# Odd layer of a two-block model: sums' reciprocals, head factors and logits by matmuls of high and low parts

## What is computed

```python
q = rms_norm(q.reshape(bsz, L, C_HEADS, C_HEAD_DIM), q_g)      # 8 heads of 128
k = rms_norm(k.reshape(bsz, L, C_KV_HEADS, C_HEAD_DIM), k_g)   # 2 heads of 128
...
logits = einsum('bqhgd,bqkhd->bqhgk', q_blk, k_sel) * (Dh ** -0.5)
logits = where(valid, logits + bias, NEG_INF)                  # bias by distance, per head
p = softmax(logits, axis=-1)
out = einsum('bqhgk,bqkhd->bqhgd', p, v_sel)
...
return (att * silu(gate)) @ w_out
```

## Time and profile before

| what | value |
|---|---|
| median of 3 runs | 2040.41 us (2038.06 to 2041.76) |
| the profiled execution's own time | 2038.71 us |
| its span | 2037.5 us |
| busy: PE, DVE, ACT, POOL | 97%, 70%, 43%, 32% |
| mean granted TensorE clock | 0.996 of full speed |
| odd attention, from the first logits' read to the last group | 833 to about 1016 us |

### The profile page before, as it was taken

How to read it: one execution, slowest core, us unless ns; L and a number is a source line. 1 busy time by engine, 2 the same in 40 slices (tenths; PEclk the granted TensorE clock), 3 DMA queues, 4 the chain that set the end, 5 groups by cost and what they waited for, 6 DMA issues and landing times.

```text
span 2037.5 us, 24547 instructions
## 1 busy us (share of the span) xinstructions
PE 1969.8 (97%) x9256; PEld 1515.3 (74%) x9256; DVE 1431.8 (70%) x2169; ACT 885.3 (43%) x1589; POOL 656.3 (32%) x476
## 2 busy tenths in 40 slices
PE   7999999999999999999999999999999999999997
PEld 6778766787648776666688777888787877778885
DVE  7667768513179997355427699899998887685539
ACT  5343366333356861344312333443326765362431
POOL 3677610452201211445444000000002673235443
PEclk9999999999999999999999999999999999999999
DMA  6322340342411122211053201121123213465322
GB/s 268 121 63 77 93 158 22 124 176 89 126 45 32 42 83 76 100 52 42 11 196 105 91 33 62 43 72 52 53 103 124 80 71 136 142 213 207 104 92 104
DMA packets 72431, 197.94 MB, mean 97 GB/s; under 512 B 11182, under 2 KB 20559, under 8 KB 71800
## 3 DMA queue, kind: packets, MB, share of 16 engines
q1 hardware_dynamic: 72168, 196.35, 28.1%
q10 hardware_dynamic: 144, 0.00, 0.0%
HBM read 152.89 MB, written 46.71 MB: 98 GB/s over the span
## 4 chain that ended last, share of the span: by engine, by line
PE 61%; DVE 19%; ACT 3%; issue 2%; POOL 1%; DMA 0%; DVEq 0%; ACTq 0%; SPq 0%
PE psum L266 58%; DVE m L2950 7%; PE psum L269 3%; DVE m L321 1%; DVE m L2971 1%; DVE m L2172 1%; DVE m L531 1%; DVE m L540 1%; DVE m L3149 1%; ACT m L301 1%; ACT m L395 1%; DVE m L3088 1%; DVE m L456 1%; DVE m L3152 1%; POOL m L311 0%
## 5 line engine op out<-in xcount | busy, mean ns | idle before, releaser
L266 PE MATMUL psum<-m,m 128*128 128x512 f32 (+9 forms) x8456 | 1886.9, 392 | 35.2 <-DVE m L321 9.5
L266 PEld LDWEIGHTS psum<-m,m 128*128 128x128 f32 (+3 forms) x8456 | 1429.0, 186 | 464.2 <-issue 145.1
L311 POOL TENSOR_TENSOR m<-m,m 128x1024 fp32r<-128x1024 f32 (+1 forms) x122 | 307.0, 2521 | 981.8 <-ACT m L301 981.5
L301 ACT ACTIVATE m<-m 128x1024 fp32r<-128x1024 f32 (+2 forms) x166 | 173.6, 1048 | 339.5 <-PE psum L266 214.9
L2950 DVE SCALAR_TENSOR_TENSOR m<-m,m,m 128x1024 f32<-128x1024 f32 x240 | 312.5, 1304 | 6.3
L269 PE MATMUL psum<-m,m 128*128 128x128 f32 x784 | 110.2, 276 | 19.3 <-ACT m L1446 6.0
L269 PEld LDWEIGHTS psum<-m,m 128*128 128x128 f32 x784 | 89.8, 141 | 39.9 <-ACT m L1446 8.0
L2172 DVE TENSOR_SCALAR_CACHE_REDUCE m<-m,m 128x896 bf16<-128x896 f32 (+4 forms) x130 | 102.8, 848 | 1.1
L2291 DVE CUSTOM_DVE_ANT_0 m<-psum,m 128x128 f32<-128x128 f32 (+3 forms) x64 | 48.3, 755 | 45.3 <-PE psum L266 22.8
L2386 ACT ACTIVATE m<-m,m 128x1024 bf16<-128x1024 f32 (+1 forms) x62 | 64.1, 1036 | 23.3 <-DVE m L2199 23.3
L2496 POOL TENSOR_TENSOR m<-m,m 128x384 f32<-128x384 f32 (+5 forms) x48 | 72.2, 1524 | 3.7 <-DVE m L2291 3.7
(11 more groups left out here) (308 smaller groups left out, 1663.0 us busy)
## 6 DMA issues: line engine op xcount, KB each, us to landing
m<-in_w SPq DMA_DIRECT2D x164, 512.0 KB, 3.4
scr_hscr<-m SPq DMA_DIRECT2D x4, 2048.0 KB, 6.6
m<-scr_hscr SPq DMA_DIRECT2D x4, 2048.0 KB, 10.5
scr_turned<-scr_strip SPq DMA_DIRECT2D x8, 575.5 KB, 12.3
m<-in_x SPq DMA_DIRECT2D x4, 1024.0 KB, 8.2
scr_gscr<-m SPq DMA_DIRECT2D x16, 256.0 KB, 4.3
m<-in_x SPq DMA_DIRECT2D x2, 2048.0 KB, 8.8
m<-scr_turned SPq DMA_DIRECT2D x8, 512.0 KB, 3.5
```

The source lines that it names most:

```text
L266: return self.nc.tensor.matmul(out, lhsT, rhs, start=start, stop=stop, skip_group_check=True)
L301: k.nc.scalar.activation(k.hi[SLOT[i]][:, 0:kk * n], k.raw[i % 2][:, 0:kk * n], ACT.Copy).then_inc(*k.up("w_hi", i))
L311: k.nc.gpsimd.tensor_tensor(lo, raw, hi.bitcast(F32), ALU.subtract).then_inc(*k.up("w_lo", i))
```

## The change

1. `norm`: `rs` is copied to fp32r into `RSP[0:64]`, and the rest goes to `RSP[64:128]`. `SEL` is the sum of two halves of the identity, so that one column picks a head's high and low rows at once. One fp32r matmul of all 128 partitions takes the place of the fp32 matmul of 10 partitions.
2. Reciprocals: DVE makes high and low parts of the four reciprocals (`RH`, `RL`) and multiplies the identity by each into `DG`, 128 x 512. PE multiplies a matrix of ones by both, two fp32r matmuls in place of four fp32 ones. `ONE` is written once by ACT.
3. Logits: `mm3` of high and low parts of queries and keys. ACT makes the high parts (`high_query`, one head ahead, 128 x 1024; `high_key`), DVE the low parts in place (`low_query`, `low_key`). A chunk of logits narrower than 256 columns is widened to 256.
4. Buffers: `pr[2]`, `strips[1]` move, and SP loads strip 1 after the last gate store and gate 0. DVE no longer waits for a gate store at unit (0, 2).

```diff
 # class Odd
+self.RSP, self.SEL = k.tile(H0 + 10 * KB, [512], F32R), k.tile(k.T0 + 512, [64], F32R)
+self.RH, self.RL = (k.tiny[:, o:o + 4] for o in (168, 172))
+self.QL, self.KL = self.MH, k.tile(PH + 32 * KB, [2, 1024], F32R)
 # tensor_odd, norm
-    hs = O.heads(half)
-    ins = k.mm(banks[half], k.ident[hs, hs.start + n:hs.start + n + 1].to_broadcast([10, 128]), O.rs[hs], True, True)
+    j = 32 * half + n
+    ins = k.mm(banks[half], O.SEL[:, j:j + 1].to_broadcast([128, 128]), O.RSP, True, True)
 # tensor_odd, s1
+pe.wait_ge(*at("q_lo", n))
+pe.wait_ge(*at("k_lo", kv))
 for c, e in O.chunks(b):
-    ins = k.mm(k.bank(bank + c // 512)[:, 0:e - c], O.QT[:, n, 128 * b:128 * b + 128], O.KT[:, n // 4, c:e], True, True)
+    e = max(e, c + 256)
+    ins = k.mm3(k.bank(bank + c // 512)[:, 0:e - c], (O.QH[n][:, bs], O.QL[:, n, bs]),
+                (O.KH[kv][:, c:e], O.KL[:, kv, c:e]), True, True)
 # tensor_odd, s3
-for i in range(4):
-    ins = k.mm(bank[:, 128 * i:128 * i + 128], O.recs[Q][:, i:i + 1].to_broadcast([128, 128]), k.ident, True, True)
+for i in range(2):
+    ins = k.mm(bank, O.ONE, O.DG[min(n, 1)][i].rearrange("p b q -> p (b q)"), i == 0, i == 1)
 # vector_odd
+def low_query(n):
+    dve.wait_ge(*at("q_hi", n))
+    V.tensor_tensor(O.QL[:, n], O.QT[:, n], O.QH[n].bitcast(F32), ALU.subtract).then_inc(*up("q_lo", n))
 if u == 18:
-    V.reciprocal(O.rs[0:64], O.rs[0:64]).then_inc(*up("head_rt"))
+    V.reciprocal(O.rs[0:64], O.rs[0:64]).then_inc(*up("head_rt", 0))
+    V.tensor_tensor(O.SEL, k.ident[:, 0:64], k.ident[:, 64:128], ALU.add).then_inc(*up("head_rt", 1))
+    V.tensor_copy(O.RSP[0:64], O.rs[0:64]).then_inc(*up("head_rt", 2))
+    V.tensor_tensor(O.RSP[64:128], O.rs[0:64], O.RSP[0:64].bitcast(F32), ALU.subtract).then_inc(*up("head_rt"))
 # vector_odd, s1b
-V.reciprocal(O.recs[Q], O.sums[Q]).then_inc(*up("od_rec", n, Q))
+V.reciprocal(O.recs[Q], O.sums[Q]).then_inc(*up("od_rec", n, Q, 0))
+V.tensor_copy(O.RH.bitcast(F32R), O.recs[Q]).then_inc(*up("od_rec", n, Q, 1))
+V.tensor_tensor(O.RL, O.recs[Q], O.RH, ALU.subtract).then_inc(*up("od_rec", n, Q, 2))
+for i, r in enumerate((O.RH, O.RL)):
+    ins = V.tensor_tensor(O.DG[min(n, 1)][i], bc(k.ident, 1, 4), bc(r, 2, 128), ALU.mult)
+ins.then_inc(*up("od_rec", n, Q))
 # vector_odd, the loop over units, ahead of s2 (scalar_odd: high_query at i % 8 == 4, high_key at i == 20)
+if i % 8 == 5 and i < 56:
+    low_query(i // 8 + 1)
+if i == 21:
+    low_key(1)
 # scalar_odd
+def high_query(n):
+    act_parts(k, O.QT[:, n], O.QH[n], "q_hi", n)
 # sync_odd
-load_strip(1)
 sp.wait_ge(*at("og_ps", 7, 1))
 load_gate(0)
+load_strip(1)
```

More of the change, by code:

```diff
@@ L190, in __init__ @@
         self.epsc = self.tile(o, [32]); o += 128
-        self.tiny = self.tile(o, [256]); o += 1024
+        self.T0, self.tiny = o, self.tile(o, [256]); o += 1024
         self.small = self.tile(o, [SM_COLS]); o += (SM_COLS * 4 + 63) // 64 * 64
@@ L1887, in __init__ @@
         self.bms = [k.tile(H0 + 4 * KB * i, [1024]) for i in range(2)]
-        self.strips = [k.tile(H0 + o * KB, [1024]) for o in (20, 8)]
-        self.pr = [k.tile(H0 + o * KB, [1024]) for o in (24, 28, 12)]
+        self.strips = [k.tile(H0 + o * KB, [1024]) for o in (20, 16)]
+        self.pr = [k.tile(H0 + o * KB, [1024]) for o in (24, 28, 8)]
+        self.QH = [k.tile(H0 + 12 * KB, [1024], F32R)] + [k.tile(X0 + (32 + 4 * n) * KB, [1024], F32R) for n in range(1, 8)]
+        self.KH = [k.tile(O + 4 * KB * i, [1024], F32R) for i in range(2)]
         self.pts = [k.tile(X0, [4, 4, 128]), k.tile(X0 + 8 * KB, [8, 4, 128])]
@@ L1895, in __init__ @@
         self.sums, self.recs = ([k.tiny[:, o + 4 * i:o + 4 * i + 4] for i in range(2)] for o in (152, 160))
+        self.RH, self.RL = (k.tiny[:, o:o + 4] for o in (168, 172))
+        self.ONE = k.tile(PH + 48 * KB + 8448, [128], F32R)
+        self.DG = [[k.tile(o + 2 * KB * i, [4, 128], F32R) for i in range(2)] for o in (X0 + 40 * KB, H0 + 12 * KB)]
         self.pairs = [4, 6]
@@ L1908, in norms_after @@
         return self.norms[u - 4:u - 3] if u >= 4 else []
-    def heads(self, half):
-        return slice(32 * half, 32 * half + 10)
     def row(self, n):
@@ L2059, in s1 @@
             pe.wait_ge(*at("head", O.norms[-1], 1))
-        pe.wait_ge(*at("head", n, b // 4))
-        for half in range(b // 4 + 1):
-            pe.wait_ge(*at("head", 8 + n // 4, half))
+        kv, bs = n // 4, slice(128 * b, 128 * b + 128)
+        pe.wait_ge(*at("q_lo", n))
+        pe.wait_ge(*at("k_lo", kv))
         bank = O.pairs[b % 2]
         for c, e in O.chunks(b):
-            ins = k.mm(k.bank(bank + c // 512)[:, 0:e - c], O.QT[:, n, 128 * b:128 * b + 128], O.KT[:, n // 4, c:e], True, True)
+            e = max(e, c + 256)
+            ins = k.mm3(k.bank(bank + c // 512)[:, 0:e - c], (O.QH[n][:, bs], O.QL[:, n, bs]),
+                        (O.KH[kv][:, c:e], O.KL[:, kv, c:e]), True, True)
         ins.then_inc(*up("od_S", n, b))
@@ L2260, in norm, with low_key @@
             *up("head", n, half, also=[("free", "od_mis", "norm", n, half)]))
+    def low_query(n):
+        dve.wait_ge(*at("q_hi", n))
+        V.tensor_tensor(O.QL[:, n], O.QT[:, n], O.QH[n].bitcast(F32), ALU.subtract).then_inc(*up("q_lo", n))
+    def low_key(kv):
+        dve.wait_ge(*at("k_hi", kv))
+        V.tensor_tensor(O.KL[:, kv], O.KT[:, kv], O.KH[kv].bitcast(F32), ALU.subtract).then_inc(*up("k_lo", kv))
     for u in range(32):
@@ L2274, in vector_odd @@
                 pick(u - 17, part)
+        if u == 27:
+            low_key(0)
+    low_query(0)
     def s1(n, b):
@@ L2295, in s1b @@
         dve.wait_ge(*at("od_exp", n, 4 * Q + 3))
-        V.reciprocal(O.recs[Q], O.sums[Q]).then_inc(*up("od_rec", n, Q))
+        if n < 2 and Q == 0:
+            dve.wait_ge(*(at("od_S", 0, 7) if n else at("og_ps", 7, 1)))
+        if n or Q:
+            dve.wait_ge(*at("od_rec_ps", *before((n, Q), 1, 2)))
+        V.reciprocal(O.recs[Q], O.sums[Q]).then_inc(*up("od_rec", n, Q, 0))
+        dve.wait_ge(*last("od_rec"))
+        V.tensor_copy(O.RH.bitcast(F32R), O.recs[Q]).then_inc(*up("od_rec", n, Q, 1))
+        dve.wait_ge(*last("od_rec"))
+        V.tensor_tensor(O.RL, O.recs[Q], O.RH, ALU.subtract).then_inc(*up("od_rec", n, Q, 2))
+        dve.wait_ge(*last("od_rec"))
+        for i, r in enumerate((O.RH, O.RL)):
+            ins = V.tensor_tensor(O.DG[min(n, 1)][i], bc(k.ident, 1, 4), bc(r, 2, 128), ALU.mult)
+        ins.then_inc(*up("od_rec", n, Q))
     def s2(n, b):
@@ L2430, in scalar_odd, with high_key @@
         act_panel(k, PANEL_AT[f"oq{m}"] + 4)
+    def high_query(n):
+        for half in range(2):
+            act.wait_ge(*at("head", n, half))
+        if n:
+            act.wait_ge(*at("og_ps", 7, 1))
+        else:
+            act.wait_ge(*at("og_out", 6))
+        act_parts(k, O.QT[:, n], O.QH[n], "q_hi", n)
+    def high_key(kv):
+        for half in range(2):
+            act.wait_ge(*at("head", 8 + kv, half))
+        if kv:
+            act.wait_ge(*at("keep", 5))
+        else:
+            act.wait_ge(*at("head_ss", 7))
+        act_parts(k, O.KT[:, kv], O.KH[kv], "k_hi", kv)
     for m in range(8):
@@ L2441, in scalar_odd @@
                 *up("og", m, half, also=[("free", "od_proj", "og", m, half)]))
+            if (m, half) == (5, 1):
+                high_key(0)
+            if (m, half) == (7, 0):
+                high_query(0)
+                A.activation(O.ONE, k.ones, ACT.Copy).then_inc(*up("od_one"))
         act_panel(k, PANEL_AT[f"og{m}"] + 4)
@@ L2469, in scalar_odd @@
             s3(O.units[i - 4][0], O.units[i - 4][1] // 4)
+        if i % 8 == 4 and i < 56:
+            high_query(i // 8 + 1)
+        if i == 20:
+            high_key(1)
         if 2 <= i <= len(O.units) + 1:
@@ L2537, in load_strip @@
         elif n == 1:
-            sp.wait_ge(*at("head_norm", O.norms[-1]))
+            sp.wait_ge(*at("og_out", 7))
         else:
```

5 lines of the change are left out of this document (3 added, 2 removed).

## The result

The changed kernel takes 2085.7 us (median of 4, 2084.29 to 2092.73), the kernel before beside it 2039.24 (2038.04 to 2041.76): a ratio of 1.0234, 95% interval 1.0212 to 1.0256. That is 2 us from the forecast of 2084 and in its range. The profiled execution was the longest of the four: 2092.73 us, span 2091.5, 54.0 above the profiled one of before.

The account below looks back on a forecast made before the run. PE, busy 97%, was taken to bound the kernel. Head 0 adds 5 us, heads 1 to 6 41, head 7 4.5, `low_key(1)` 1.1, less 7.1 for factors: +44.5, so 2084 us beside the median; range 2050 to 2100.

Parts of the forecast that it names:

- The forecast case: Attention: DVE's new instructions, cast included, and POOL's hold each other, PE waits for DVE; 2084 us, chance 0.40.
- What PE saves: PE's fp32r matmuls: 2.5 us a head less in attention where PE sets the pace, 7.1 us gained on head factors.
- Factors: Half panels with a `norm`: ten times 0.84 us saved on PE, less 1.3 for DVE's longer list: 7.1 us gained.
- What is in the way: Attention: DVE's new two-input instructions and casts alternate with POOL's, each paying for a whole POOL instruction.
- the sign that the prediction gave: Profile after: DVE's new multiplications and subtraction would have means of 1.5 to 2.5 us, not 0.2 and 0.68.
- The middle of a head: First set alternates with POOL's sums of 768, 896 and 1024; read of block 5 starts 5.2 us late, at 9.6.
- Group 0 and the end of a head: Group 0's multiplication at 15.25, second set ending 6.05 us later, next head's at 29.4: 6.8 us a head more.
- `low_key`: DVE's low part of the second group of keys, `low_key(1)`, in attention: 1.1 us added once.
- (1): Attention: DVE and POOL don't hold each other; period 21.4 us, 2023 us in all, faster; chance 0.10.
- (2): Attention: held, but the cast is free; 1.25 us a head less than forecast, 2074 us; chance 0.26.
- (3): Attention: held, but DVE reaches its sets in POOL's pauses; half the loss, 2055 to 2060 us; chance 0.10.
- (4): Attention: PE idles about 9 us a head and its clock falls, costing 2 us a head: 2100 us; chance 0.08.

Follow-up runs that it names:

- E2: Kernel before with the change's head factors and logits, reciprocals made as before: 2043.41 us, ratio 1.0010 to the kernel before.
- E1: Changed kernel with fp32 logits and fp32 reciprocals again, only the head factors in high and low parts: 2037.68 us, 0.9978 of the kernel before.
- E9: Changed kernel plus 12 unused fp32r matmuls a head (heads 1 to 7) ahead of PE's wait for the read of block 5: 2076.39 us, 1.0174.
- E3: Changed kernel with fp32 logits and no high or low queries and keys, factors and reciprocals still changed: 2089.05 us, 1.0228 to the kernel before.
- E4: Changed kernel, each DVE product of identity and reciprocals split into four 128x128 pieces with one SBUF tensor input and an unused accumulator: 2081.42 us, 1.0189.
- E5: Changed kernel with POOL's sums of bias and mask replaced by memsets to zero: 2054.05 us, 1.0056 to the kernel before.
- E10: Changed kernel with the reciprocals' cast and products made by ScalarE, DVE keeping reciprocal and rest: 2050.45 us, 1.0040 to the kernel before.
- E11: Changed kernel with reciprocals' cast and products on ScalarE, most low parts of queries and keys moved into DVE's wait for the group 1 product: 2037.21 us, 0.9978.

## Why the prediction was right, and where it was not

**Size and sign.** +46.5 us by the medians, +44.5 forecast. The forecast case happened: holding, with PE waiting for DVE. (2040.41 + 44.5 is 2084.9; the prediction says 2084.) The experiments price the parts by their ratios: factors -0.22%, logits +0.3% (E2 over E1), reciprocals +2.2% (the change over E2), of which +0.6% is the clock (over E9). That the sum came out so near is luck in part: errors of up to 2.4 us a head, told below, offset one another. In the profiled execution head 0 adds 5.9 us (5 forecast), heads 1 to 6 with `low_key(1)` 42.1 (41 and 1.1) and head 7 6.0 (4.5); but that execution is 7.0 us above the median.

**What PE saves.** Factors: -7.1 forecast; -5.7 in the stage, in the change's profile and in E1's (88.19 us in both). A half panel with a `norm` takes 825.59 - 819.64 = 5.95 us, as forecast; the term was too large for what DVE gives back, since at one place PE now waits 1.49 us for DVE's head. E1's median is 3.5 us lower. Logits and reciprocals: rightly taken as no gain where DVE sets the pace; with fp32 logits (E3) the ratio is 1.0228, with the change's 1.0234.

**What is in the way.** Right in kind: each kind of new instruction paid for POOL's work that ran, the cast too (0.87 us mean, 1.89 longest, for 0.17 of work). The size was below the sign that the prediction gave, means of 1.5 to 2.5 us: the products have 1.28 and the rest 1.07. The Trainium skill (SBUF — State Buffer, "Who interferes with whom") says that copy and cast can contend as well. That now has its row: the trace agrees.

**The middle of a head: the step that failed.** I let the second product wait for POOL's sum of 1024, and put the read of block 5 at +9.6. It comes at +7.27 (932.25 - 924.98). That sum writes the tile that the read of block 5 uses, so POOL waits for DVE there: "[2.10 <-DVE m L2315]". Two sums, not three, could hold the set. The sum of 1024 is held by `low_query` after it, 3.06 us for 2.13. This made the forecast 2.3 us too long at that read, and 2.4 in a head at full clock: E9's period is 27.0.

**Group 0 and the end of a head.** L2353 at +14.24 (15.25 forecast), where PE and no longer DVE is last (a wait of 1.01 us at a clock of 0.79). The second set ends +5.77 behind it (6.05). Then PE's stretch to the product takes 8.76 us in this head (8.74 and 8.75 in two others), and not what full clock gives, 7.06 (in E9, and in the heads between). The clock is in the +14.24 as well: in E9 the same event comes at +13.27. So what the misplaced sum had too much, the clock took back: the mean period of heads 1 to 6 is (1041.17 - 863.73) / 6 = 29.57, forecast 29.4.

**`low_key`.** 1.1 us forecast, 6 in E2: it was priced at its bare length, though it stands among POOL's sums, and what its wait does to the clock was not priced at all. In the change itself it is held as long as in E2 (kernel after):

```profile
902.77 3.15 DVE L2278 TENSOR_TENSOR m<-m,m 128x1024 fp32r<-128x1024 f32 x1
```

Its head takes 924.98 - 893.50 = 31.5 us: 1.7 more than the longer ones beside it, but its last stretch of PE is at full clock (7.06 us), and against the heads that have that too (28.3) it is 3.2 more. That is the holding of `low_key` and its own work. E2's second part, the fall of the clock, is no extra here: PE's matmuls of that place are at a lowered clock in the heads beside it too (16 in 5.86 us from 933.25).

**Rivals.** (1), no holding, is excluded by the rows of E4, E5 and E10; but its world can be built: E11 does the change's arithmetic and is 0.2% faster. (2), a free cast, is excluded by the cast's row. (3), sets in POOL's pauses, did not occur in its size: the sets take 4.98 and 3.95 us for 1.7 of work. In one place it did: the second product ran while POOL waited for DVE. (4), the clock, was partly true, together with the forecast: 9 us by E9, where I gave it 16 and only as an alternative. That was a mistake of form: a fall of the clock adds to holding, and should have been a term of the sum.

What stays open: why heads alternate between periods of 28.3 and 29.8 us (28.4 and 30.1 in E3). The longer ones have PE's last stretch at a lowered clock, and the rows don't show why only every other one has. And a set with nothing held on DVE wasn't run: E5 still holds the cast, E10 the rest.

## What to carry to other kernels

A DVE instruction of two SBUF inputs, or a cast, that stands where POOL works can cost as much as POOL's instruction, whatever its own size (here 1.56 us for 128x4 elements, 0.16 where nothing holds them). In such a stage, put small preparatory work on ScalarE, or where DVE waits for PE anyway, before judging the arithmetic that needs it. When a chain of engines is stretched, look for PE's gaps and their clock as a cost that comes on top. And for each instruction thought to be in the way, check whether it is free to start at all: its output buffer may be what the waiting engine still reads.

## What was not expected of the hardware

- A POOL memset, which reads nothing, holds a DVE cast: 1.94 us for 0.17 of work, through a POOL instruction and two memsets after it (E5). The Trainium skill (SBUF — State Buffer, "Who interferes with whom") says that VectorE in a two-port mode, which a cast can enter, and GpSimd exclude each other, and that whoever issues first gets the shared ports for the whole instruction. That the cast is blocked agrees; the order doesn't: the cast was issued at 934.77, the memsets ran from 935.16. Beside sums, the cast issued during a POOL instruction went ahead of the next one (0.49 and 0.45 us).
- Not every DVE instruction with two SBUF inputs was held: 128x4 elements took 1.56 us behind a running sum, and 1024 columns took their bare 1.21, since they started first, and POOL's sum paid for it (3.06 us for 2.13; 2.13 again in E3, which has no `low_query`). Here the price went by who was running, not by size.
- 84 matmuls without use made the kernel 9 us faster (E9), with DVE's set as long as before: the granted clock of the attention rose from 0.90 to 0.98.
- The clock can cost as much as the delay ahead of it: in E2 `low_key`, 3.1 us, came with PE's next 16 matmuls 2.9 us longer (6.20 for 3.32, granted clock 0.52).
